# The gates' projection and the bonus moved out of the projection stage and into the slots of an RWKV-7 scan

## The reference

```python
h_in = rms_norm(x, norm1_w)
z = h_in @ w_in                       # 2048 x 12064
z_attn, z_rwkv, z_gate = jnp.split(z, cuts, axis=-1)
# attention: 24 heads of 64 in three dilated windows -> o_attn, 512 x 512
# RWKV-7: token shift, LoRA inputs, one delta-rule scan per direction, GroupNorm
bonus = jnp.sum(jnp.sum(r_h[None] * k_dir * r_k, axis=-1, keepdims=True) * v_h[None], axis=0)
o_rwkv = (gn + bonus.reshape(b, s, RWKV_WIDTH)) * gate      # 512 x 1024
gates = jax.nn.sigmoid(z_gate.reshape(b, s, N_BRANCHES, D_MODEL) + b_gate)
branch_a = o_attn @ w_branch_attn
branch_b = o_rwkv @ w_branch_rwkv
merged = gates[:, :, 0] * branch_a + gates[:, :, 1] * branch_b
x = x + merged @ w_out
x = x + (silu(h2 @ w_ffn_gate) * (h2 @ w_ffn_up)) @ w_ffn_down      # h2 = rms_norm(x)
```

## Time and profile before

| | |
|---|---|
| Time, median of 3 runs | 4070.27 us (4060.76 to 4073.32) |
| The profiled execution's own time | 4070.06 us, its span 4068.3 us |
| TensorE busy | 3607.9 us (89%), mean granted clock 0.923 |
| PEld busy | 2929.7 us (72%) |
| VectorE busy | 1544.4 us (38%) |
| ScalarE busy | 1091.1 us (27%) |
| GpSimd busy | 1759.6 us (43%) |
| DMA | 402.57 MB, 33.9% of the 16 engines' span |

### The profile page before, as it was taken

How to read it: one execution, slowest core, us unless ns; L and a number is a source line. 1 busy time by engine, 2 the same in 40 slices (tenths; PEclk the granted TensorE clock), 3 DMA queues, 4 the chain that set the end, 5 groups by cost and what they waited for, 6 DMA issues and landing times. The chain is left out here.

```text
span 4068.3 us, 45482 instructions
## 1 busy us (share of the span) xinstructions
PE 3607.9 (89%) x16462; PEld 2929.7 (72%) x16462; DVE 1544.4 (38%) x1818; ACT 1091.1 (27%) x1656; POOL 1759.6 (43%) x1397
## 2 busy tenths in 40 slices
PE   5999999899997774677776889999999999999999
PEld 4477788677775552567675568788888888888887
DVE  3066615651001235777772525533123203312321
ACT  4322211212222332344442222322122213212221
POOL 2033344334442002888885454344444444444443
PEclk8699999999998556898988999999999999999999
DMA  4333344344542101323332443333333333333333
GB/s 156 131 101 98 103 125 124 96 122 141 158 143 93 47 23 37 70 64 73 66 71 65 146 142 110 102 93 97 92 106 97 88 100 101 90 92 107 93 91 105
DMA packets 747784, 402.57 MB, mean 99 GB/s; under 512 B 180814, under 2 KB 703242, under 8 KB 747178
## 3 DMA queue, kind: packets, MB, share of 16 engines
q1 hardware_dynamic: 747690, 401.38, 33.9%
HBM read 343.64 MB, written 57.67 MB: 99 GB/s over the span
## 5 line engine op out<-in xcount | busy, mean ns | idle before, releaser
L131 POOL TENSOR_TENSOR w_lo_b<-w_raw_b,w_hi_b 128x2048 fp32r<-128x2048 f32 (+3 forms) x200 | 747.5, 3738 | 1005.8 <-ACT w_hi_b L124 1005.6
L131 POOL TENSOR_TENSOR w_lo<-w_raw,w_hi 128x2048 fp32r<-128x2048 f32 x95 | 437.8, 4609 | 788.3 <-ACT w_hi L124 788.3
L140 PE MATMUL f_bank<-act_rounded,w_lo_b 128*128 128x512 f32 x1664 | 649.8, 391 | 16.2 <-POOL act_rounded L1776 8.4
L141 PE MATMUL f_bank<-act_rounded,w_hi_b 128*128 128x512 f32 x1664 | 649.2, 390 | 0.0
L142 PE MATMUL f_bank<-act_rounded,w_hi_b 128*128 128x512 f32 x1664 | 648.9, 390 | 0.0
L140 PE MATMUL bank<-h_hi,w_lo 128*128 128x512 f32 x1520 | 609.8, 401 | 29.8 <-POOL w_lo L131 23.1
L142 PE MATMUL bank<-h_hi,w_hi 128*128 128x512 f32 x1520 | 596.8, 393 | 0.0
L141 PE MATMUL bank<-h_lo,w_hi 128*128 128x512 f32 x1520 | 596.6, 392 | 0.0
L124 ACT CAST w_hi_b<-w_raw_b 128x2048 fp32r<-128x2048 f32 (+3 forms) x200 | 313.0, 1565 | 946.8 <-PE f_bank L142 876.2
L140 PEld LDWEIGHTS f_bank<-act_rounded,w_lo_b 128*128 128x128 f32 x1664 | 313.4, 188 | 83.0 <-POOL act_rounded L1776 8.8
L140 PEld LDWEIGHTS bank<-h_hi,w_lo 128*128 128x128 f32 x1520 | 288.7, 190 | 106.1 <-issue 30.5
(11 more groups left out here) (311 smaller groups left out, 4431.0 us busy)
## 6 DMA issues: line engine op xcount, KB each, us to landing
w_raw<-in_w_in_dram SPq DMA_DIRECT2D x95, 1024.0 KB, 5.4
w_raw_b<-in_w_ffn_gate_dram SPq DMA_DIRECT2D x44, 1024.0 KB, 5.2
w_raw_b<-in_w_ffn_up_dram SPq DMA_DIRECT2D x44, 1024.0 KB, 5.2
w_raw_b<-in_w_ffn_down_dram SPq DMA_DIRECT2D x64, 704.0 KB, 4.5
zt<-out SPq DMA_DIRECT2D x92, 256.0 KB, 4.1
w_raw_b<-in_w_out_dram SPq DMA_DIRECT2D x16, 1024.0 KB, 6.1
zt<-lout SPq DMA_DIRECT2D x40, 256.0 KB, 2.0
b_in<-zt SPq DMA_DIRECT2D x40, 256.0 KB, 4.5
```

The costliest lines, as they stand in the source:

```text
L131: pool.tensor_tensor(g.w_lo[n.slot][:, 0:k, :], g.w_raw[n.slot][:, 0:k, :], g.w_hi[n.slot][:, 0:k, :].bitcast(F32), ALU.subtract).then_inc ...
L140: pe.matmul(bank, wl, hi[:, ka, :], start=start and j == 0, stop=False)
L141: pe.matmul(bank, wh, lo[:, ka, :], start=False, stop=False)
```

## The change

The last 32 slabs and the bonus leave the projection. In each of the slots -5 to 26 of the scan TensorE now makes one gate slab, slab c = slot + 5, with all its 48 matmuls behind the stage ts. Weights come in halves of 8 k tiles (0.5 MB): SyncE loads them, ScalarE rounds one half ahead of its stage tk and one at the slot's end, and VectorE (not GpSimd) makes the low part in four pieces of 128x512, at the start of the slot, ahead of qg, ahead of operands and ahead of state. At the start of the next slot ScalarE copies the slab from PSUM, and SyncE stores it to `zt` without the sigmoid.

The bonus is made in 16 pieces of half the tokens' width, one in every second slot: four operations of VectorE ahead of decays, the matmul behind akv, the product behind state. To make room, `AHEAD` goes from 5 to 4, the tiles `ari` and `xin` become one, `xar`, the copy `low` becomes a transfer, and attention's result goes to DRAM (`oat`) and is split in the output phase. VectorE's qg becomes two operations. In the output phase ScalarE puts the sigmoid on the gates, in place, behind the rounding of the weights of slab m + 2 (`gate_a`, `gate_b`), and the products with the gates wait for it. The diff's core:

```diff
-    NA, NB, ND = 36, 24, 32
-    SA0, SB0, SD0, SEND = C0, C0 + NA, C0 + NA + NB, C0 + NA + NB + ND
+    NA, NB = 36, 24
+    SA0, SB0, SEND = C0, C0 + NA, C0 + NA + NB
...
-                def bonus_loads(row, so_far):
-                    sp.wait_ge(b_ready, so_far)
-                    for k, first in enumerate((ROW_RKV, ROW_RKV + RW, ROW_RKV + 2 * RW, ROW_IC, ROW_IC + RW)):
-                        sp.dma_start(b_in[:, k, :], zt[bass.ds(row + first, P), :]).then_inc(b_landed, 16)
-                def bonus_store(row, count):
-                    sp.wait_ge(b_ready, count)
-                    sp.dma_start(zt[bass.ds(row + ROW_BONUS, P), :], bonus[:, :]).then_inc(b_stored, 16)
...
-                section(SD0, ND, COL_GATES, ROW_MIX, mix_ready, SD0, [None, None, None], pairs=True)
-                sp.wait_ge(b_stored, 16 * NPAIR)
...
-                def mix(st, row_tile):
-                    act.wait_ge(g.w_used, st.count())
-                    act.wait_ge(g.out_stored[st.slot], st.slot_count(2) - 16 * (C0 // 2 + (0 if st.slot else 1)))
-                    act.activation(out[st.slot][:, :], bank[st.slot][:, :], ACT.Sigmoid, bias=row_tile).then_inc(mix_ready, 1)
-                with act.Fori(0, ND // UN - 1) as i:
-                    for j in range(UN):
-                        mix(Step(SD0 + j, i, UN), g.params[:, bass.ds(i * UN + (PARAMS["b_gate"][0] + j), 1)])
-                        split_hi(act, g, Step(SD0 + j + 2, i, UN), KD)
...
-AHEAD = 5
+AHEAD = 4
...
+GATE_TILES = {"ts": 16}
...
-ACT_SLOT = (("x1", "u"), ("low", "v"), ("ta", "v"), ("tb", "v"), ("wx", "u"), ("ux", "u"), ("tk", "v"), ("tv", "v"),
+ACT_SLOT = (("x1", "u"), ("ta", "v"), ("tb", "v"), ("wx", "u"), ("ux", "u"), ("tk", "v"), ("tv", "v"),
...
+def slab_in(slot):
+    return slot + AHEAD + 1
+def bonus_in(g):
+    return (g - 1) // 2 if g % 2 and (g - 1) // 2 < 2 * NPAIR else None
...
+                def weights(h):
+                    if h >= RAW_RING:
+                        sp.wait_ge(w_used, h - RAW_RING + 1)
+                    c, k = h // 2, (h % 2) * KH
+                    sp.dma_start(raw_half(w_raw, h), w_in[:, k:k + KH, COL_GATES + c * P:COL_GATES + (c + 1) * P]).then_inc(w_landed[h % RAW_RING], 16)
...
+                for slot in SLOTS:
                     u, v, w = (unit_at(slot, x) for x in "uvw")
+                    c = slab_in(slot)
+                    if 2 * c + 4 < 2 * NGATE:
+                        weights(2 * c + 4)
...
+                    if 1 <= c <= NGATE:
+                        sp.wait_ge(gate_taken, c)
+                        sp.dma_start(zt[ROW_MIX + (c - 1) * P:ROW_MIX + c * P, :], gate[(c - 1) % 2][:, :]).then_inc(gate_stored[(c - 1) % 2], 16)
...
+                            for e in range(2):
+                                at = CH * e
+                                sp.dma_start(low[s][at:at + HALF, :, at + HALF:at + CH],
+                                             nb[it % 4, s, :, at:at + HALF, HALF:CH].rearrange("q i t -> i q t")).then_inc(d_landed[s], 16)
...
+                    if 2 * c + 5 < 2 * NGATE:
+                        weights(2 * c + 5)
                     if 0 <= w < NUNIT - 1:
                         sp.wait_ge(taken_dve, DVE_AT["operands", w])
                         load(w + 1)
...
+                    if c % 2 == 0:
+                        b = c // 2
+                        if 1 <= b <= 2 * NPAIR:
+                            sp.wait_ge(b_ready, b)
+                            sp.dma_start(bonus_rows(b - 1, ROW_BONUS), bonus[:, :]).then_inc(b_stored, 16)
+                        if b < 2 * NPAIR:
+                            for i, row in enumerate((ROW_RKV, ROW_RKV + RW, ROW_RKV + 2 * RW, ROW_IC, ROW_IC + RW)):
+                                sp.dma_start(b_in[:, i, :], bonus_rows(b, row)).then_inc(b_landed, 16)
...
+                def high(h):
+                    if h < 2 * NGATE:
+                        act.wait_ge(w_landed[h % RAW_RING], 16 * (h // RAW_RING + 1))
+                        if h >= HI_RING:
+                            act.wait_ge(w_used, h - HI_RING + 1)
+                        act.copy(hi_half(h), raw_half(w_raw, h)).then_inc(hi_ready, 1)
+                for h in range(3):
+                    high(h)
+                for slot in SLOTS:
+                    c = slab_in(slot)
+                    if 1 <= c <= NGATE:
+                        act.wait_ge(w_used, 2 * c)
+                        if c >= 3:
+                            act.wait_ge(gate_stored[(c - 1) % 2], 16 * ((c - 1) // 2))
+                        act.copy(gate[(c - 1) % 2][:, :], gbank[(c - 1) % 2][:, :]).then_inc(gate_taken, 1)
...
+                        if name == "tk":
+                            high(2 * c + 3)
...
+                    high(2 * c + 4)
...
+                def low_part(h, q):
+                    if h >= 2 * NGATE:
+                        return
+                    if q == 0:
+                        dve.wait_ge(hi_ready, h + 1)
+                    r = slice(q * (KH // 2), (q + 1) * (KH // 2))
+                    ins = dve.tensor_tensor(raw_half(w_lo, h)[:, r, :], raw_half(w_raw, h)[:, r, :], hi_half(h)[:, r, :].bitcast(F32), ALU.subtract)
+                    if q == 1:
+                        ins.then_inc(lo_ready, 1)
...
+                def bonus_terms(b):
+                    dve.wait_ge(b_landed, 80 * (b + 1))
+                    dve.tensor_tensor(b_in[:, 3, :], b_in[:, 3, :], b_in[:, 4, :], ALU.add).then_inc(b_chain, 1)
...
+                def bonus_out(b):
+                    dve.wait_ge(b_summed, b + 1)
...
+                    dve.tensor_tensor(bonus[:, :], b_in[:, 2, :], gbank[0][:, 0:HS], ALU.mult).then_inc(b_ready, 1)
...
+                        if name == "decays" and bonus_in(c) is not None:
+                            bonus_terms(bonus_in(c))
+                        if name == "qg":
+                            low_part(2 * c + 2, 1)
+                        if name == "operands":
+                            low_part(2 * c + 3, 0)
+                        if name == "state":
+                            low_part(2 * c + 3, 1)
...
-                            dve.tensor_tensor(qg[:, :, :], ari[st][:, :, CH:3 * CH], bank[2][:, :, :], ALU.add).then_inc(taken_dve, 1)
+                            dve.tensor_tensor(qg[:, :, 0:CH], xar[st][:, :, P:3 * CH], bank[2][:, :, 0:CH], ALU.add)
+                            dve.tensor_tensor(qg[:, :, CH:P], eyes, bank[2][:, :, CH:P], ALU.add).then_inc(taken_dve, 1)
...
+                def gate_tile(c, k):
+                    h, kk = 2 * c + k // KH, k % KH
+                    if k == 0:
+                        if c >= 2:
+                            pe.wait_ge(gate_taken, c - 1)
+                            if c % 2 == 0:
+                                pe.wait_ge(b_ready, c // 2)
+                    if kk == 0:
+                        pe.wait_ge(lo_ready, h + 1)
+                    wh, wl, o = hi_half(h)[:, kk, :], raw_half(w_lo, h)[:, kk, :], gbank[c % 2][:, :]
+                    pe.matmul(o, wl, g.h_hi[:, k, :], start=k == 0, stop=False)
+                    pe.matmul(o, wh, g.h_lo[:, k, :], start=False, stop=False)
+                    ins = pe.matmul(o, wh, g.h_hi[:, k, :], start=False, stop=k == KD - 1)
+                    if kk == KH - 1:
+                        ins.then_inc(w_used, 1)
...
+                        if has_stage(name, n):
+                            stage(name, n, n % 2, n % NSET)
+                        if c < NGATE:
+                            for k in range(k, k + GATE_TILES.get(name, 0)):
+                                gate_tile(c, k)
+                            k += 1 if name in GATE_TILES else 0
+                        if name == "akv" and bonus_in(c) is not None:
+                            b = bonus_in(c)
+                            pe.wait_ge(b_chain, 4 * b + 4)
+                            pe.wait_ge(gate_taken, min(c, NGATE))
+                            pe.matmul(gbank[0][:, 0:HS], g.head_ones[:, :], b_in[:, 0, :], start=True, stop=True).then_inc(b_summed, 1)
...
-                act.copy(g.oa_hi[:, j, :], oa_f[:, j, :]).then_inc(oh_ready, 1)
...
+                sp.wait_ge(o_ready, j + 1)
+                sp.dma_start(oat[j], oa_f[:, j, :]).then_inc(oa_stored, 16)
...
                         attn_slab(0)
+                        sp.dma_start(oa_f, oat.rearrange("k p n -> p k n")).then_inc(oa_landed, 16)
                         attn_slab(1)
...
+                def gate_a(m):
+                    act.wait_ge(mix_landed[m % 2], 16 * (m // 2 + 1))
+                    act.activation(mix[m % 2], mix[m % 2], ACT.Sigmoid, bias=param(g, "b_gate", m)).then_inc(mix_ready, 1)
+                def gate_b(i, j):
+                    act.wait_ge(mix_landed[j], i * 16 + (16 * (KD // 2) + 16))
+                    act.activation(mix[j], mix[j], ACT.Sigmoid,
```

(9 more changed lines are left out.)

456 lines of the change are left out of this document (232 added, 224 removed).

## The result

The changed kernel takes 4110.75 us (median of 4 runs, 4102.79 to 4115.03), the kernel before 4069.72 us (4 runs in the same comparison). The ratio is 1.0102, with a 95% interval of 1.0078 to 1.0125: slower by one per cent. The forecast was 4074 us with a range of 4032 to 4115, so the time lies inside the range and on the side that had 0.35.

A forecast was written before the change was run, and what follows sets the result against it. Prediction: TensorE bounds the projection's and output's slabs; the scan is a chain of engine waits that a slab behind ts does not shorten. Terms -362 - 2 + 19 + 309 + 9 + 31 = +4 on 4070 us: 4074, range 4032 to 4115.

The forecast's parts named there:

- The projection, attention: Projection loses 32 gate slabs and eight bonus pairs, -362 us; end of attention trades its high/low split for stores, -2.
- The slab stands where TensorE does not wait: Scan slot: a slab behind ts shortens none of the waits inside the slot and adds its 10.8 us.
- A slot without bonus, 28.6 us: Scan slot: chain of 16.8 us, slab 10.8, clock loss 1.0; x1 to yh taken as 10.6.
- The bonus, 2.7 us: Every second scan slot: four VectorE operations ahead of decays delay yh by 2.7 us, bounds 1.8 and 4.
- VectorE becomes the slot's chain: Slower rival: scan slots lose 1.5 us more, +40, 4114 us; sign: decays to qg over 5.2 us without bonus; chance 0.26.
- The slots together, 810 us: Scan slots 0 to 26: 27 x 28.6 + 14 x 2.7 = 810 us against 501, +309, bounds +269 and +346.
- GpSimd's pace: Scan before the change: inversions at 18.1 us a slot co-determine the slots' 18.55 us; with slabs this limit is gone.
- The end, +9: Scan's tail: last inversion starts only in slot 27, so x1 of slot 30 comes 49 us after slot 27's; +9.
- The output, +31: Output phase: sigmoids lengthen two chains, attention branch +24 (gates every 5.5 us), branch slabs +7; bounds +10 and +50.
- the slower rival: The rival "VectorE becomes the slot's chain", in the scan's slots: +40, 4114 us, chance 0.26.
- The rule on the clock: Scan slots: a slot 85% busy could be expected to get a clock nearer 1.00, giving back 27 us.
- the clock stays up: Faster rival: the dense half of each scan slot keeps the clock up, 4047 us, chance 0.19.

The follow-up runs named there:

- e4: Changed kernel with only 2 of each gate slab's 16 k tiles multiplied (gates come out wrong): 3952.27 us, ratio 0.9724 to the kernel before.
- e3: Changed kernel with each slab's 16 k tiles spread over the slot (3 behind tb, 1 tv, 3 akv, 9 ts): 3978.37 us, ratio 0.9784.
- e11: Changed kernel with all 16 tiles of the slab behind tb, ahead of qg, none behind ts: 4008.83 us, ratio 0.9854.
- e2: Changed kernel with the bonus's four VectorE operations moved behind operands and its matmul into the slab: 4047.96 us, ratio 0.9956.
- e10: Kernel before with half of GpSimd's steps of each inversion left out (outputs come out wrong): 4050.1 us, ratio 0.9947.
- e7: Kernel before with AHEAD = 4 in place of 5 and nothing else: 4071.05 us, ratio 1.0017.
- e1: Changed kernel with the output phase's gate sigmoids ahead of the rounding of the weights of slab m + 2: 4063.43 us, ratio 0.9981.
- e9: e2 with 3 of the slab's tiles behind tb and 13 behind ts, the gap before ts left open: 3980.98 us, ratio 0.9793.
- e5: Changed kernel with the edits of e1, e2 and e3 together: 3862.75 us, ratio 0.9482.
- e8: e5 with 3 tiles behind tv and 7 behind ts in place of 1 and 9: 3852.83 us, ratio 0.9475.

## Why the prediction came out as it did

- **The projection, attention.** Right, within 6 and 1 us.
- **"The slab stands where TensorE does not wait."** Right. e4's slots without bonus show that the slab covers nothing there, e3 and e11 that the same slabs elsewhere cost 107 to 128 us less. It is the main reason why 368 us taken out bring nothing.
- **A slot without bonus, 28.6 us.** Measured 28.45 in the slot shown, by two errors that cancel: to yh it is 9.7 us and not 10.6, since decays end in time and the part of `w_lo` before qg lies in VectorE's wait for TensorE. The clock costs 1.9 us and not 1.0. On average these slots take 28.0 us.
- **The bonus, 2.7 us.** Mis-sized, and beyond its bound of 4: 4.4 us between the two slots that are shown. yh starts 3.4 us later (2.5 for the terms, the rest for operations stretched beside GpSimd). From yh to ts it is 2.6 us longer, most of it at the lower clock, and the slab is 1.6 us shorter since the clock does not fall in it. The rival "VectorE becomes the slot's chain" (decays to qg over 5.2 us) did not come by its own sign: 3.8 us from decays to qg in the slot without bonus that is shown. Its mechanism, that what stands ahead of qg delays yh, came in the slots with bonus: e2 gets 63 us back by the place alone. So VectorE's order was at fault, not its load.
- **The slots together, 810 us against 820.** So near by luck. At the measured averages the bonus costs 65 us and not 38, 27 more, and 27 slots without it are 17 us shorter than the forecast's 772.
- **GpSimd's pace.** "Co-determines them" is wrong, by e10. No term of the sum hung on it, but the 18.1 us that agreed with the average were taken for a cause; with half of GpSimd's work the slots fell by 14 us of 501.
- **The end, +9.** The step that it worked out is right to the microsecond: x1 of slot 30 behind the last inversion, forecast 49 us after x1 of slot 27 and measured 49.15 (40.3 before). What it put at nothing is slot 30 behind that wait, 16.7 us at a clock of 0.55 in place of 11.2 at 1.00. Together 14.5, and AHEAD's alone (e7).
- **The output, +31: a step that failed, and the largest part of the difference.** For the attention branch the forecast traced the sigmoid behind the rounding, behind the weights, behind the gate of the pair before, and got 5.5 us a gate; measured 5.3 to 5.6 for eight of the last eleven, 5.9 to 7.4 for the others, 24.5 us more from the first gate to the last. (Its two parts, 15 and 7, make 22 and not the 24 that it wrote.) For the RWKV branch it counted only ScalarE's 1.05 and 0.63 us, "+7", though the order there is the same: rounding, sigmoid, and weights issued behind the gates' load. Measured +30. It is 23 of the 40 us by which the forecast was low, and e1 gives it back. The other 17 are the slots (10), the end (5.5), the prologue (4) and the rest of the output (4), less 7 in projection and attention.
- **The time of 4114 us** that the slower rival gave is near the measured one, but by another mechanism for over half of it. It is not evidence for that rival.

**The rule on the clock.** The slots with a slab kept a granted clock of 0.90 (windows above), as before, and none of the 27 us came back: in both slots shown it fell once. e2 and e9 show that such gaps need not cost the clock every time: with the same gap or gaps in each slot, it fell in some and not in others (26.9 or 28.3 us; 24.8 or 26.4). The Trainium skill ("TensorE: Matmul & The Clock Gate", section "HAM oscillation — how this bites in real kernels") describes a loop whose wait for data makes the clock fall in every pass; the waits that it tells of are longer than the 1.9 us here, so these loops are not its case, and the clock fell in many of their passes all the same. Without gaps (e5, e8) the clock was 1.00 in every slot but the first of e5. But e11's slots without bonus kept one gap of 1.9 us and were at 1.00 too. So the rival "the clock stays up" did not come with a busier slot alone; closing the gaps, or one of them (e11), brought it. What decides whether a gap costs the clock stays open.

## What to carry to other kernels

In this kernel dense work that was moved into a latency-bound loop paid only where it stood in a gap. So first look for the gaps of the engine in one pass of the loop, and put it there in pieces. Against the slot of 17.99 us before, the same 48 matmuls cost 10.5 us at the end of the slot (28.45), 6.7 us in one block in the first large gap (24.7, e11) and 4.5 us spread over its gaps (22.51). And when an instruction is put into an in-order queue, read what stands ahead of it there, what that waits for, and who issues it: one sigmoid behind one rounding cost 48 us in two loops, and the loop that was traced was forecast to a tenth of a microsecond in most passes, while the one that was only counted was off by 23 us.

With the three moves (e5, e8) the same change is 5.2% faster than the kernel before, not 1% slower.

## What the runs showed of the hardware

Executions of the same first stage differ by up to 20 us, and go with the time at which the granted clock rises. Windows of the projection's start, of the kernel before and of e1, whose code is the same there:

```profile
140.00:150.00 10.00, 9.87 (x12) 2.89 (x12) 0.00 (x0) 2.42 (x4) 0.00 (x0) 0.50 0.34 131
...
170.00:180.00 10.00, 10.00 (x19) 5.12 (x18) 0.00 (x0) 2.45 (x3) 0.00 (x0) 0.53 0.38 121
```

```profile
140.00:150.00 10.00, 9.87 (x18) 2.76 (x16) 0.00 (x0) 3.08 (x6) 0.00 (x0) 0.81 0.41 157
...
170.00:180.00 10.00, 10.00 (x46) 8.29 (x45) 0.69 (x1) 2.43 (x2) 4.60 (x1) 1.00 0.00 0
```

TensorE is busy in both, but the granted clock rises from 0.50 some 35 us later in the first. It does so at 143 to 144 us in five of the thirteen traces (e1, e7, e8, e9, e10) and at 179 to 181 in the other eight. Attention's first load comes at 916 to 920 us in seven of the ten kernels that share the changed one's projection, and at 902 us in three (e1, e8, e9); with the projection of before it comes at 1285 us, and at 1265 and 1269 in e7 and e10. This is why stages are compared here, and not spans. Why the clock rises late in one execution and not in another stays open.
